# Issuing the half swaps of v and g from SyncE instead of ScalarE in a state-space recurrence

## What is computed

```
z = rmsnorm(x) @ w_in                     # 1056 x 2048 by 2048 x 6152
u = z[:, OFF_U:OFF_GS]                    # 64 groups of 16 channels
bu = einsum(b_bar, u)                     # 64 complex states a group
hs = scan over t of  h[t] = a_bar * h[t-1] + bu[t]
y  = real(einsum(c, hs)) + d_skip * u
y  = gelu(y) * sigmoid(gelu(y) @ w_glu)
out = concat(attention * silu(ga), y * silu(gs)) @ w_out ...
```

## Time and profile before

| | |
|---|---|
| median of three runs | 2520.17 us (2510.91, 2520.17, 2522.29) |
| profiled execution | 2515.18 us, span 2513.5 us |
| PE busy | 2275.2 us, 91% |
| DVE busy | 1584.9 us, 63% |
| ACT busy | 787.4 us, 31% |
| DMA queues | q1: 267.17 MB; q0: 77.95 MB; q10: 43.20 MB |
| DMA rate | 155 GB/s mean over the span |

### The profile page before, as it was taken

The page is one execution under the profiler, slowest core; times in us unless marked ns, Lnnn a source line. Parts: engine busy times, 40 slices in busy tenths (PEclk is TensorE's granted clock), DMA queues, the critical chain, the costliest instruction groups (busy, mean ns, idle before and its releaser), DMA issues. The chain is left out here.

```text
span 2513.5 us, 43261 instructions
## 1 busy us (share of the span) xinstructions
PE 2275.2 (91%) x16025; PEld 2142.0 (85%) x16025; DVE 1584.9 (63%) x2910; ACT 787.4 (31%) x1660; POOL 316.8 (13%) x350
## 2 busy tenths in 40 slices
PE   3799999999799998999878886896999999999996
PEld 3799999999799998999857775795888888999996
DVE  4777767766687776777457863744445665434663
ACT  6342333333434444333256543211001113001112
POOL 0011000000111111111143313300001110001110
PEclk9899999999899999999989997898999999999998
DMA  7375344444656776876275615345445436444332
GB/s 232 97 220 170 112 127 145 143 134 131 257 181 181 200 209 193 229 208 199 70 233 170 188 63 187 122 153 168 119 114 167 116 106 205 112 117 122 106 105 98
DMA packets 399413, 390.28 MB, mean 155 GB/s; under 512 B 73897, under 2 KB 341705, under 8 KB 392801
## 3 DMA queue, kind: packets, MB, share of 16 engines
q1 hardware_dynamic: 343776, 267.17, 36.8%
q0 software_dynamic: 20704, 77.95, 9.0%
q10 hardware_dynamic: 34784, 43.20, 5.6%
HBM read 257.56 MB, written 122.01 MB: 151 GB/s over the span
## 5 line engine op out<-in xcount | busy, mean ns | idle before, releaser
L739 PE MATMUL acc<-t_act,w_hi 128*128 128x264 f32 x5376 | 898.5, 290 | 40.7 <-DVE zb L1301 10.6
L739 PEld LDWEIGHTS acc<-t_act,w_hi 128*128 128x128 f32 x5376 | 759.3, 192 | 48.2 <-issue 47.0
L739 PE MATMUL acc<-t_act,w_lo 128*128 128x264 f32 x2688 | 553.5, 288 | 0.0
L2598 PE MATMUL post_acc<-region_hi,w_post_hi 128*128 128x272 f32 (+1 forms) x1536 | 418.3, 327 | 24.5 <-DVE region_lo L2707 19.8
L739 PEld LDWEIGHTS acc<-t_act,w_lo 128*128 128x128 f32 x2688 | 423.3, 192 | 0.0
L2598 PE MATMUL post_acc<-region_hi,w_post_lo 128*128 128x272 f32 (+1 forms) x1536 | 415.4, 325 | 0.0
L2598 PE MATMUL post_acc<-region_lo,w_post_hi 128*128 128x272 f32 (+1 forms) x1536 | 414.8, 324 | 0.0
L1294 DVE TENSOR_TENSOR w_lo<-w_raw_f,w_hi 128x512 fp32r<-128x512 f32 x288 | 198.3, 689 | 198.0 <-ACT w_hi L947 196.9
L2598 PEld LDWEIGHTS post_acc<-region_hi,w_post_hi 128*128 128x128 f32 x1536 | 258.3, 189 | 50.5 <-issue 16.1
L2598 PEld LDWEIGHTS post_acc<-region_lo,w_post_hi 128*128 128x128 f32 x1536 | 258.4, 189 | 21.8
L2598 PEld LDWEIGHTS post_acc<-region_hi,w_post_lo 128*128 128x128 f32 x1536 | 257.1, 189 | 22.5
(11 more groups left out here) (379 smaller groups left out, 3229.3 us busy)
## 6 DMA issues: line engine op xcount, KB each, us to landing
w_raw_f<-in_w_in_dram SPq DMA_DIRECT2D x96, 512.0 KB, 4.2
w_raw<-in_w_out_dram SPq DMA_DIRECT2D x64, 512.0 KB, 4.8
w_raw<-in_w_pg_dram SPq DMA_DIRECT2D x64, 512.0 KB, 4.8
cT<-zb SPq DMA_DIRECT2D x24, 1056.0 KB, 4.4
zb<-cT POOLq DMA_DIRECT2D x96, 264.0 KB, 5.3
zT<-zb POOLq DMA_DIRECT2D x80, 264.0 KB, 3.7
eT<-e_out ACTq DMA_DIRECT2D x16, 528.0 KB, 2.8
t_act<-tS POOLq DMA_DIRECT2D x7, 1056.0 KB, 10.5
```

The costliest lines, as they stand in the source:

```text
L739: mm = pe.matmul(out[:, c, 0:QN], w[:, k, :], t_act[:, SIDE[r], x, k, c * QN:(c + 1) * QN], start=(opens and k == 0 and m == 0), stop=(k = ...
L2598: mm = pe.matmul(acc[b][:, c, 0:width], w[:, k, :], a[region][:, k, start:start + width], start=(k == 0 and n == 0), stop=(k == KD - 1 and ...
```

## The change

The four swap DMAs of each block leave ACT's program and enter SP's. The one for `v` goes behind the loads of the readout weights and ahead of the second weight half; the one for `g` goes behind the first weight half of pass p+2 and ahead of the y stores. SP takes over the waits: for `v_copied`, for `scanned`, and for `v_used`. ACT no longer waits for its own copy nor for DVE's scan.

```diff
--- before.py
+++ after.py
@@ -500,6 +500,21 @@
                     sp.wait_ge(v_done, q)
                 sp.dma_start(ws_in[:], d["w_state"][:, q * PB:(q + 1) * PB, :]).then_inc(ws_loaded, 16)
 
+            def swap(x, landed):
+
+                sp.dma_start(x[0:ST, 1], x[ST:P, 0]).then_inc(landed, 16)
+                sp.dma_start(x[ST:P, 1], x[0:ST, 0]).then_inc(landed, 16)
+
+            def swap_v(q):
+                sp.wait_ge(v_copied, q + 1)
+                swap(v, v_swapped)
+
+            def swap_g(q):
+                sp.wait_ge(scanned, q + 1)
+                if q:
+                    sp.wait_ge(v_used, q)
+                swap(g, g_swapped)
+
             def load_ro(q):
                 if q:
                     sp.wait_ge(y_done, q)
@@ -533,6 +548,8 @@
                     load_rot(q)
                 if 2 <= q <= NPB + 1:
                     load_ro(q - 2)
+                if 0 <= q - 1 < NPB:
+                    swap_v(q - 1)
                 load_w(p + 1, 1)
                 if 1 <= p <= NP:
                     store_part(p - 1)
@@ -544,6 +561,8 @@
                 if 0 <= q < NPB:
                     load_u(q)
                 load_w(p + 2, 0)
+                if 0 <= q - 1 < NPB:
+                    swap_g(q - 1)
                 if p < RIDES:
                     if p == 0:
                         sp.wait_ge(t_ready, 7)
@@ -1028,11 +1047,6 @@
                 nc.scalar.copy(kern[:, :, L - 1:, :].rearrange("p g k c -> p g (k c)"),
                                bank_c[0:GC, :].rearrange("p (g x) -> p g x", g=PB)).then_inc(k_copied, 1)
 
-            def swap(x, landed):
-
-                act.dma_start(x[0:ST, 1], x[ST:P, 0]).then_inc(landed, 16)
-                act.dma_start(x[ST:P, 1], x[0:ST, 0]).then_inc(landed, 16)
-
             def copy_v(q):
                 act.wait_ge(v_done, q + 1)
                 if q:
@@ -1041,14 +1055,6 @@
                     s = nc.scalar.copy(v[:, 0, 2 * h:2 * h + 2],
                                        oth[:, h, 0:2 * NJ].rearrange("p (g j) -> p g j", g=2))
                 s.then_inc(v_copied, 1)
-                act.wait_ge(v_copied, q + 1)
-                swap(v, v_swapped)
-
-            def swap_g(q):
-                act.wait_ge(scanned, q + 1)
-                if q:
-                    act.wait_ge(v_used, q)
-                swap(g, g_swapped)
 
             def keep_ends(q):
 
@@ -1101,8 +1107,6 @@
                 if 0 <= q - 1 < NPB:
                     if j == 0:
                         copy_v(q - 1)
-                    if j == 6:
-                        swap_g(q - 1)
                 if 0 <= q - 2 < NPB:
                     if j == 2:
                         keep_ends(q - 2)
```

## The result

The changed kernel takes 2544.3 us at the median of 6 runs (2534.3 to 2553.47), against 2520.86 us for the kernel before (6 runs, 2510.91 to 2527.35). The medians are 23 us apart. The ratio, which is estimated by itself and not taken from the medians, is 1.0107, with a 95% interval of 1.0081 to 1.0133, which makes 27 us. So the change costs 23 to 27 us, where 8 us had been forecast. The profiled execution is the slowest of the six, with a span of 2551.8 us.

A forecast was written before the change was run, and what follows sets the result against it. PE was taken to set the pace, idling 16.0 us early and 7.6 us late. ACT 0, early half 0 to 1 and late half 8 made about +8 us on the 2520.17 us median: 2528 us, range 2514 to 2545.

The forecast's parts named there:

- as costed at 0: ACT losing four issues a block: its wait for PE stays, copies and casts keep their times, 0 us.
- One sign: In the profile after, ACT's waits for PE were to grow by the issue time it lost.
- I take the emptier engines: Late half: transfers ahead of v mostly drained, a half swap lands in 5.7 us, v 1.1 us later a pass, 8 us.
- the ring: Late passes: rotation, scan, g, y stores, loads and v's landing form a loop that must close once a pass.
- the upper end of 7.4 us: Late half, v's issue to rotation at the present median landing: 0.5 + 6.8, and 0.1 to the rotation.
- the transfers ahead of v are the same in number: Late half: only the transfers' order changes, so what the swap waits for is mostly drained at its later issue.
- If the landing time stays as it is: Late half: v 4.4 us later in the worked pass, ring 26.2 to 27.6 us, 15 to 25 us in all.
- rival A: Late half: ring closes with present landing times and becomes bound by SP, +15 to +25 us, 2535 to 2545; chance 0.33.
- rival D: Late half: DVE or PE wait for weights or `wr_in`, at most 33 us, with A; chance 0.05.
- the two readings that stood in the prediction: Swap of v behind SP's loads: own queue gives it a turn, so the sum grows; or issuer costs only issue time, unchanged.

The follow-up runs named there:

- The run with the earlier loads: Changed kernel, both swaps still on SP, with readout weights and turns loaded one step earlier, ahead of the wait for the scan: 2516.3 us, ratio 1.0002.
- the slowest experiment: Changed kernel with the swap of v moved ahead of SP's four loads (state weights, turns, readout weights): 2559.84 us, ratio 1.0177.

## Why the prediction was wrong

**The direction of the argument held.** Nothing came back from ACT: its row behind the copy of v still waits for PE, as costed at 0. SP became late by the wait for the scan, v was issued 3.4 us behind its copy in the pass shown (4.4 forecast), the y stores begin 1.5 us behind the scan's end, PE's waits for `u2` are 14.6 us in 7 passes (some 12 forecast), and the early half grew by no more than two profiles differ (238.6 against 235.3 us to the first late `states` group). One sign did not come: ACT's waits for PE did not grow by the issue time (0.71 us in the pass shown, 1.31 in the earlier trace rows).

**The step that failed: the landing.** "I take the emptier engines" let a half of v land in 5.7 us and the rotation start 6.3 us behind v's issue, so that v would be 1.1 us later a pass. The halves land in 7.0 us at the median, and the rotation starts 8.4 us behind the issue on average (7.0 to 10.2 in the seven late steps of the table above). That is 2.1 us a pass too little, 15 us over seven steps; every other term of the ring was right within 0.3 us. The rows of the kernel before had it: there the rotation starts 8.5 us behind the issue on average in the same seven blocks. Even the upper end of 7.4 us was low, because it took the median of all halves where the rotation waits for the second one.

The reason I gave was that POOL's loads would get ahead while SP was late. In the pass shown POOL issued three of them from 1119.49 and a fourth at 1122.07:

```profile
1110.26 0.55 POOL L649 DMA_DIRECT2D zT<-zb  x1 [13.77 <-DVE zb L1314]
...
1119.49 1.61 POOL L663 DMA_DIRECT2D zb<-cT  x3
1122.07 0.54 POOL L663 DMA_DIRECT2D zb<-cT  x1 [0.97 <-DMA zT<-zb]
```

In the kernel before, behind the three in the earlier trace rows:

```profile
1106.48 0.54 POOL L644 DMA_DIRECT2D zb<-cT  x1 [2.43 <-DMA zT<-zb]
```

The first three are issued 4.2 us ahead of v at 1123.67, against 0.8 us in the earlier trace rows. So they did get ahead, and in that pass the rotation came 7.1 us behind the issue rather than 9.6; but that pass is the second shortest of the seven. The fourth load was issued 3.2 us behind v before and is now ahead of it. So "the transfers ahead of v are the same in number" does not hold. That this is what keeps the landing long is argued; no run isolates it.

**The ring was right.** "If the landing time stays as it is" gave a ring of 26.2 to 27.6 us and 15 to 25 us in all. It takes 26.8 us, and the recurrence is 21.6 us longer in the profiles. This was rival A, with 0.33 and 2535 to 2545 us, and it should have been the forecast. The run with the earlier loads bears it out: with the two readout loads and the turns taken out of the ring, the late rotations are 24.0 us apart again and the loss is gone.

**A cost set to nothing that was not.** The lateness of the readout weights was only in rival D, with 0.05. It is a way of its own: with v on time PE idles 9.5 to 10.7 us ahead of the readout. In the changed kernel itself it is 4.9 us, 2 us more than before. The costs don't add up: g alone costs 13 us, v alone nothing, both together 27. The pair costs more than its parts since v is late only when SP is.

**The clock was left out of the sum.** In the changed kernel, around the longest of PE's waits for `u2`:

```profile
1077.00:1080.00 3.00, 0.54 (x5) 0.34 (x4) 2.50 (x5) 0.00 (x0) 0.00 (x0) 1.00 0.51 110
1080.00:1084.00 4.00, 3.52 (x17) 3.55 (x18) 4.00 (x12) 0.60 (x1) 0.55 (x1) 0.57 0.43 128
1084.00:1087.00 3.00, 3.00 (x27) 3.00 (x27) 2.80 (x8) 1.19 (x3) 0.55 (x1) 1.00 0.27 99
```

```profile
1080.48 0.78 PE L758 MATMUL acc<-t_act,w_hi 128*128 128x264 f32 x2 [2.94 <-DVE zb L1305]
```

PE was busy 0.54 of 3 us, then resumes at 1080.48 and gets 0.57 of the clock until 1084, mostly the lower level of 1.2 GHz. The Trainium skill, TensorE: Matmul & The Clock Gate, section "Part 1: The HAM clock gate (the "warmup" mystery)", says that the throttled state is the default and activity releases it; the trace agrees in that PE's clock falls after this idling and returns while it works. Yet most of this is no cost on top of the ring. The late window has three such slow stretches; the first, at 982, lies ahead of the late steps that the ring bounds. In the other two, behind the waits that ended at 1080.48 and 1133.84, ACT's next copy of v ends 1.4 to 1.5 us later after the rotation than in the other passes, but still 1.9 and 2.0 us before SP issues v. With the ring setting the pace, slower matmuls fill time in which PE would otherwise idle; only the scan ends 0.2 to 0.3 us later.

**The rule of the queue.** The run with v alone on SP separates the two readings that stood in the prediction. It lands v in 6.6 and 6.9 us (two profiles) behind SP's loads against 6.8 us on ACT's queue. The Trainium skill, DMA: Bandwidth & Descriptors, section "Issuing engines are not separate DMA queues", says that issuing from several engines only saves the sequencer's time for the issue. The trace agrees by these landings; turns between the queues made no difference that can be seen while SP is on time.

**What stays open.** Why the landing did not shorten, and why v lands later still with g behind the y stores, no run shows; a run that moves POOL's loads alone is missing. The profiled execution is also 15 us longer behind the recurrence (38.3 us of span, of which 23.6 us by the last `states` group, 1145.9 to 1169.5). I did not follow these; the execution is the slowest of six that spread over 19 us.

## What to carry to other kernels

Here a DMA moved to another issuer cost nothing by the queue that it stood in, and much by what the new issuer's program waits for. Before moving one, write down what the new issuer waits for just ahead, everything that it issues behind, and whether that work leads back to the same wait: a ring like this must close within a pass, and it was 2.5 us too long (26.8 against 24.3). Price the landing in such a ring by the time from issue to first use in the present trace (8.5 us), not by the shortest landing seen (5.7 us). If the ring is too long, take other work out of the ring first (loads whose buffers are already free can go ahead of the wait); here that alone undid the whole loss.

## What the runs showed of the hardware

A wait of PE can cost more than its length. Around an idle of 4.67 us the granted clock was 0.55 over 7 us, behind one of 2.94 us 0.57 over 4 us. The length alone does not decide it: in the late half of the kernel before an idle of 2.86 us left the clock at 1.00, and in that of the changed kernel one of 2.19 us, ended at 1133.84, was followed by the lower level while one of 2.18 us, ended at 1162.75, was not.

```profile
992.61 0.46 PE L839 MATMUL oth<-u_in,toep_in 128*128 128x132 f32 x2 [2.86 <-issue]
```

```profile
994.00:997.00 3.00, 3.00 (x27) 3.00 (x27) 2.50 (x7) 0.26 (x1) 0.41 (x1) 1.00 0.68 245
```

In the early half of the slowest experiment, with six waits of 4.0 to 4.9 us, the mean clock was 0.90 against 0.96.

A half swap of 135 KB landed in the same time from either queue (6.6 and 6.9 us against 6.8 at the median) beside the same traffic, while in the early half it took 2.6 us. The DMA rate there is hardly lower (199 against 217 GB/s); what differs is what stands close to the swap. In a late pass POOL's three loads are issued 0.8 us ahead of it, in an early one the swap is issued at 902.17 and POOL's loads from 909.59. With SP's readout loads moved away (the kernel before with the earlier loads) it landed in 5.9 us. That POOL's loads make up the rest is argued, no run moves them.
